# A mixture-of-experts stage on one core: a pair's 128 slots divided 32 and 96, with column tiles of 32, 32 and 64

## The reference

```python
grp = argmax(h @ w_grp + b_grp)                  # 4 groups of 8 experts
p_in, top_i = top_k(softmax(logits in the group), 2)
gate = p_grp * p_in / sum(p_in)
expert = grp * 8 + top_i                         # 2 experts of 32 for each of 256 tokens
# for each expert e, over the tokens sent to it (blocks padded to 128):
y = (silu(x @ w_gate[e]) * (x @ w_up[e])) @ w_down[e]     # 1024 -> 512 -> 1024
# the result of a token is the sum of its two experts' y, each times its gate;
# then a residual with a gain, and a last norm
```

## Time and profile before

| | us |
|---|---|
| median of 3 runs | 1170.4 |
| the profiled execution | 1173.7 |
| its span, first to last instruction | 1172.0 |
| PE busy (a matmul record counts from its start to its modelled end) | 1073.6 (92%) |
| PE weight loads | 606.6 (52%) |
| DVE busy | 399.2 (34%) |
| ACT busy | 169.7 (14%) |
| DMA, mean rate over the span | 263 GB/s |

### The profile page before, as it was taken

The page is one execution under the profiler, slowest core; times in us unless marked ns, Lnnn a source line. Parts: engine busy times, 40 slices in busy tenths (PEclk is TensorE's granted clock), DMA queues, the critical chain, the costliest instruction groups (busy, mean ns, idle before and its releaser), DMA issues.

```text
span 1172.0 us, 12847 instructions
## 1 busy us (share of the span) xinstructions
PE 1073.6 (92%) x5189; PEld 606.6 (52%) x5189; DVE 399.2 (34%) x735; ACT 169.7 (14%) x366; POOL 29.6 (3%) x88
## 2 busy tenths in 40 slices
PE   5999989789999999989977889999999988888885
PEld 4776877537666666478555363333333332232322
DVE  2857652404222222330033254443322222222223
ACT  1131330300000000010055000001011000000001
POOL 5300000000000000000000000000000000000000
PEclk9999965798999999999989979999999999999999
DMA  8442000065666666664410346999999999999993
GB/s 355 180 150 72 3 2 0 13 275 201 271 275 276 277 275 277 278 243 169 163 72 1 131 164 279 419 428 428 428 429 427 427 428 429 428 429 428 427 425 141
DMA packets 26816, 308.38 MB, mean 263 GB/s; under 512 B 6138, under 2 KB 6296, under 8 KB 7192
## 3 DMA queue, kind: packets, MB, share of 16 engines
q1 hardware_dynamic: 25308, 307.58, 63.4%
q10 hardware_dynamic: 1468, 0.24, 0.1%
HBM read 306.76 MB, written 1.05 MB: 263 GB/s over the span
## 4 chain that ended last, share of the span: by engine, by line
PE 75%; DMA 15%; DVE 6%; ACT 2%; issue 1%; SPq 0%; DVEq 0%
PE PS L1546 11%; PE PS L1005 11%; PE PS L1375 9%; PE PS L1389 9%; PE PS L1000 8%; DMA slot<-in_moe_w_up_dram 7%; PE PS L1592 7%; DMA AR<-in_moe_w_up_dram 4%; DMA XH<-in_moe_w_up_dram 4%; PE PS L1562 4%; PE PS L1232 2%; PE PS L1537 1%; PE PS L1174 1%; PE PS L1221 1%; PE PS L1480 1%; DVE AR L2013 1%
## 5 line engine op out<-in xcount | busy, mean ns | idle before, releaser
L1546 PE MATMUL PS<-slot,ATT 128*64 128x512 f32 (+1 forms) x672 | 142.7, 574 | 17.1 <-DMA slot<-in_moe_w_up_dram 12.5
L1375 PE MATMUL PS<-XH,slot 128*128 128x256 f32 x512 | 111.6, 379 | 0.0
L1389 PE MATMUL PS<-slot,AR 128*128 128x512 f32 x256 | 111.2, 592 | 0.0
L1375 PEld LDWEIGHTS PS<-XH,slot 128*128 128x128 f32 x512 | 97.3, 190 | 16.2 <-issue 3.3
L1546 PEld LDWEIGHTS PS<-slot,ATT 128*64 128x64 f32 x672 | 48.2, 137 | 110.0 <-issue 88.9
L1000 PE MATMUL PS<-XH,slot 128*128 128x256 f32 x432 | 96.0, 385 | 2.2 <-DVE XH L1694 1.2
L1000 PEld LDWEIGHTS PS<-XH,slot 128*128 128x128 f32 x432 | 83.3, 194 | 14.6 <-DVE XH L1694 1.6
L1389 PEld LDWEIGHTS PS<-slot,AR 128*128 128x128 f32 x256 | 48.6, 190 | 58.2 <-issue 57.9
L1546 PE MATMUL PS<-AR,ATT 128*64 128x512 f32 x320 | 72.0, 595 | 7.4 <-DMA AR<-in_moe_w_up_dram 5.0
L1592 PE MATMUL PS<-slot,MASKS 128*64 128x512 f32 x320 | 70.9, 595 | 1.3 <-DVE AR L2195 1.3
L1005 PE MATMUL PS<-slot,XH 128*128 128x256 f32 (+4 forms) x224 | 70.8, 475 | 0.0
(11 more groups left out here) (389 smaller groups left out, 1007.1 us busy)
## 6 DMA issues: line engine op xcount, KB each, us to landing
slot<-in_moe_w_up_dram SPq DMA_DIRECT2D x20, 2048.0 KB, 35.7
slot<-in_moe_w_down_dram SPq DMA_DIRECT2D x20, 2048.0 KB, 36.4
slot<-in_moe_w_gate_dram SPq DMA_DIRECT2D x18, 2048.0 KB, 32.7
slot<-in_w_ffn_dram SPq DMA_DIRECT2D x16, 2048.0 KB, 9.9
AR<-in_ada_w_dram SPq DMA_DIRECT2D x16, 1536.0 KB, 10.7
AR<-in_moe_w_gate_dram SPq DMA_DIRECT2D x11, 2048.0 KB, 36.3
AR<-in_moe_w_up_dram SPq DMA_DIRECT2D x9, 2048.0 KB, 35.0
AR<-in_moe_w_down_dram SPq DMA_DIRECT2D x9, 2048.0 KB, 30.6
```

The lines of the kernel that those rows point to most:

```text
L1375: ins = pe.matmul(PS[:, 2 * j + f // 2, (f % 2) * T:(f % 2 + 1) * T], slots[s][:, c * 512 + f * P:c * 512 + (f + 1) * P], HT[:, c, :], sta ...
L1389: ins = pe.matmul(PS[:, 4 + 2 * i + n, :], AT[:, j, f * T + i * P:f * T + (i + 1) * P], slots[s][:, f * D + n * 512:f * D + (n + 1) * 512] ...
L1546: ins = pe.matmul(PS[k * CAP:(k + 1) * CAP, bank_, 0:n], HS[:, c, k * CAP:(k + 1) * CAP], w[:, at:at + n], start=(c == 0), stop=(c == KC - 1))
```

## The change: what it does

- Of a pair's 128 slots, 32 (`FEW`) go to the expert with fewer tokens and 96 (`MANY`) to the other, and the smaller one always stands on the first side. Which one it is comes from a comparison of the counts on DVE (`SWAP`, and as integers `SIDE`). Pair 0 keeps 64 and 64 and its order.
- SP reads two sides for each pair from `SIDE` and fetches each unit in two DMAs, one for each side, 8 KB in each partition, so that the smaller expert's weights come into columns 0 to 2047 of the buffer. A unit's semaphore counts 32 for 16. Pair 0 and pair 1's units 10 and 11 are issued with the sides (0, 1) (pair 1's order is never changed: `swap[:, 0:2]` is cleared). SP waits once for `side_ready`, behind unit 11.
- DVE works out places, keys and gates in the order of the sides (`PLACE`, `KEYP`, `WTP`), ahead of pair 0's selections.
- PE does each step for pairs 1 to 15 in three matmuls: slots 0 to 31 with the first side's weights, 32 to 63 and 64 to 127 with the second side's (`SKEWED`). Each moves 512 columns.
- ACT copies 32 and 96 token columns for 64 and 64, and reads the two places after its wait for up.
- Further passes hold what goes over 32, 96 or (pair 0) 64, by 64s. The number of possible passes is 8 where it was 7.

```diff
 CAP = 64
+FEW, MANY = 32, 96
+NP = NE // 2
...
-        OVN = T * 2 // (CAP + 1)
+        OVN = 8
...
+            def pair_side(kind, half, pair, side):
+
+                src = kinds[kind][half].rearrange("q p (k n) -> q k p n", k=2)
+                return src[bass.ds(pair, 1), bass.ds(side, 1)].rearrange("q k p n -> p (q k n)")
+
+            def ring(u, g=0, sides=(0, 1)):
 
                 kind, half = u % UP // 2, u % 2
-                sp.dma_start(RING[u % NR], kinds[kind][half, bass.ds(PERIOD * g + u // UP, 1)].rearrange("q p n -> p (q n)"))\
-                    .then_inc(ring_loaded[u % NR], 16)
+                for k in range(2):
+                    sp.dma_start(RING[u % NR][:, k * HALF:(k + 1) * HALF], pair_side(kind, half, PERIOD * g + u // UP, sides[k]))\
+                        .then_inc(ring_loaded[u % NR], 16)
...
+            def pair_units(q, g):
+
+                sides = [sp.value_load(SIDE[0:1, bass.ds(2 * (PERIOD * g + q) + k, 1)], min_val=0, max_val=1) for k in range(2)]
+                for u in range(UP * q, UP * q + UP):
+                    ring_unit(u, g, sides)
+
+            for u in range(NR, 2 * UP):
+                ring_unit(u, 0, (0, 1))
+            sp.wait_ge(sems["side_ready"], 1)
+            for q in range(2, PERIOD):
+                pair_units(q, 0)
...
+            def expert_tokens(m):
+
+                few, many = place(2 * m), place(2 * m + 1)
+                act.activation(HS[:, :, 0:FEW], sorted_from(few, FEW), ACT.Copy)
+                act.activation(HS[:, :, FEW:P], sorted_from(many, MANY), ACT.Copy).then_inc(sems["hs_ready"], 1)
...
-                pe.wait_ge(ring_loaded[u % NR], 16 * (UP * PERIOD // NR * g + u // NR + 1))
+                pe.wait_ge(ring_loaded[u % NR], 32 * (UP * PERIOD // NR * g + u // NR + 1))
                 return RING[u % NR]
 
+            EQUAL = ((0, CAP, 0), (CAP, P, 1))
+            SKEWED = ((0, FEW, 0), (FEW, 2 * FEW, 1), (2 * FEW, P, 1))
+
+            def product(bank_, tiles, w, at, src, start, stop):
+
+                for r0, r1, k in tiles:
+                    ins = pe.matmul(PS[r0:r1, bank_, :], src[:, r0:r1], w[:, k * HALF + at:k * HALF + at + 512], start=start, stop=stop)
+                return ins
...
+                    for c in range(4 * half, 4 * half + 4):
+                        ins = product(4 + kind, tiles, w, c % 4 * EFF, HS[:, c, :], c == 0, c == KC - 1)
+                    ins.then_inc(sems[names[half]], 1)
...
+                            ins = product(6 + n, tiles, w, f * D + n * 512, AC[:, 2 * half + f, :], half == 0 and f == 0,
+                                          half == 1 and f == 1)
...
+            step(tt(swap, c_a, c_b, ALU.is_gt))
+            step(dve.memset(swap[:, 0:2], 0.0))
+            step(ts(kept, swap, -1.0, 1.0, ALU.mult, ALU.add))
+            dve.tensor_copy(ab(SIDE)[:, 0, :], swap)
+            dve.tensor_copy(ab(SIDE)[:, 1, :], kept).then_inc(sems["side_ready"], 1)
+            step(tt(d, s_b, s_a, ALU.subtract))
+            step(tt(d, d, swap, ALU.mult))
+            tt(ab(lo_hi)[:, 0, :], s_a, d, ALU.add)
+            step(tt(ab(lo_hi)[:, 1, :], s_b, d, ALU.subtract))
+            step(ts(lo_hi, lo_hi, float(HSS_AT), None, ALU.add))
+            dve.tensor_copy(PLACE[:, 0:NE], lo_hi).then_inc(sems["place_ready"], 1)
...
+            step(tt(dd, k_b, k_a, ALU.subtract))
+            step(tt(dd, dd, by(swap), ALU.mult))
+            tt(side_of(KEYP, 0), k_a, dd, ALU.add)
+            tt(side_of(KEYP, 1), k_b, dd, ALU.subtract)
+            for k, (x, y) in enumerate(((w_a, w_b), (w_b, w_a))):
+                step(tt(ww, y, by(swap), ALU.mult))
+                step(tt(side_of(WTP, k), x, by(kept), ALU.mult))
+                step(tt(side_of(WTP, k), side_of(WTP, k), ww, ALU.add))
...
-            selections(0).then_inc(sems["selw_ready"], 1)
+            selections(0, CAP).then_inc(sems["selw_ready"], 1)
...
-                selections(m + 1).then_inc(sems["selw_ready"], 1)
+                selections(m + 1, FEW).then_inc(sems["selw_ready"], 1)
```

More of the change, by code:

```diff
@@ L522, in _, with ring_unit @@
             ring(9)
-            def ring_unit(u, g):
+            def ring_unit(u, g, sides):
                 before = u - NR
                 sp.wait_ge(sems[released[before % UP]], PERIOD * g + before // UP + 1)
[L528 to L536, removed]
+                ring(u, g, sides)
+            def pair_units(q, g):
[7 more added lines that the diff above has]
+                pair_units(q, 0)
+            with sp.Fori(1, NP // PERIOD) as g:
+                for q in range(PERIOD):
+                    pair_units(q, g)
+            pair_units(0, NP // PERIOD)
             sp.wait_ge(sems["over_ready"], 1)
@@ L547, in _ @@
                         for half in range(2):
[L548 to L550 removed]
+                            sp.dma_start(OVER[kind][:, half * HALF:(half + 1) * HALF], pair_side(kind, half, pair_of, side))\
                                 .then_inc(sems[("over_gate", "over_up", "over_down")[kind]], 16)
@@ L928, in _ @@
             act.wait_ge(sems["place_ready"], 1)
-            at = places(1)
             act.wait_ge(sems["hss_filled"], KC)
-            expert_tokens(at)
-            with act.Fori(1, NE // 2 - 1) as m:
-                at = places(m + 1)
+            expert_tokens(1)
+            with act.Fori(1, NP - 1) as m:
                 expert_copies(m, EFF)
@@ L944, in _ @@
                     act.wait_ge(sems["up_filled"], x + NE // 2)
-                    expert_tokens(places(x + NE // 2))
+                    further_tokens(x)
                     expert_copies(x + NE // 2, EFF // 2)
@@ L1589, in project_back @@
                         for f in range(2):
[L1590 to L1593, removed]
+                            ins = product(6 + n, tiles, w, f * D + n * 512, AC[:, 2 * half + f, :], half == 0 and f == 0,
+                                          half == 1 and f == 1)
                     ins.then_inc(sems[("down_half", "down_filled")[half]], 1)
             pe.wait_ge(sems["first_low"], 1)
-            project(0, 0, 0, ("gate_half", "gate_filled"))
-            project(0, 0, 1, ("up_half", "up_filled"))
+            project(0, 0, 0, ("gate_half", "gate_filled"), EQUAL)
+            project(0, 0, 1, ("up_half", "up_filled"), EQUAL)
             pe.wait_ge(sems["sels_ready"], 1)
@@ L2108, in _ @@
             ins.then_inc(sems["sels_ready"], 1)
-            def selections(pair):
+            ab = lambda t: t.rearrange("p (q k) -> p k q", k=2)
+            side_of = lambda t, k: t.rearrange("p i (q k) -> p i k q", k=2)[:, :, k, :]
+            (c_a, c_b), (s_a, s_b) = ((ab(t)[:, 0, :], ab(t)[:, 1, :]) for t in (counts, first))
+            swap, kept = SWAP[:, 0, :], SWAP[:, 1, :]
+            d, lo_hi = E32[:, 4, 0:NP], E32[:, 5, 0:NE]
+            step(tt(swap, c_a, c_b, ALU.is_gt))
+            step(dve.memset(swap[:, 0:2], 0.0))
@@ new lines, in _ @@
+            k_a, k_b, w_a, w_b = (side_of(t, k) for t in (KEY, WT) for k in range(2))
+            by = lambda t: bc(t, 1, NT)
+            dd, ww = (E32[:, k, 0:NT * NP].rearrange("p (i q) -> p i q", i=NT) for k in (6, 7))
+            step(tt(dd, k_b, k_a, ALU.subtract))
[6 more added lines that the diff above has]
+                step(tt(side_of(WTP, k), side_of(WTP, k), ww, ALU.add))
@@ L2112, in selections @@
+            def selections(pair, few):
                 for i in range(NT):
[L2113 to L2116, removed]
+                    for k, (r0, r1) in enumerate(((0, few), (few, P))):
+                        ins = ts(SELW[:, i, r0:r1], IOTA[:, 0:r1 - r0], KEYP[:, i, bass.ds(2 * pair + k, 1)],
+                                 WTP[:, i, bass.ds(2 * pair + k, 1)], ALU.is_equal, ALU.mult)
@@ L2184, in further_experts @@
                 dve.tensor_copy(OVI[:, OVN + 1:2 * OVN + 1], side)
+                step(tt(first, first, CAPS, ALU.add))
                 step(stt(first, start, -float(CAP), first, ALU.mult, ALU.add))
```

84 lines of the change are left out of this document (47 added, 37 removed).

## The result

| | before | changed |
|---|---|---|
| median (lowest to highest) | 1171.5 us (1170.4 to 1176.7, 4 runs) | 1524.9 us (1522.6 to 1526.2, 4 runs) |
| ratio of the times, 95% interval | | 1.300 [1.295, 1.304] |
| span of the profiled execution | 1172.0 us | 1520.9 us |
| mean granted TensorE clock | 0.953 | 0.969 |

The account below looks back on a forecast made before the run. Transfers bound later pairs before, PE after: pair 1's start at 734.79, 15 pairs of 52.1 us (781.5), 5.1 to the scatter's end and 8.5 for the norm give a 1530 us span, forecast 1530 us, range 1154 to 1550.

Parts of the forecast that it names:

- What bounds it, before and after: Experts' stage: transfers set later pairs before at 29.4 us, PE having 4.4 us to spare; after the change PE is the bound.
- at half or less: Sign of being right: in the experts' stage the slices show DMA at half or less and PE near full.
- The step: PE's 32, 32 and 64 wide matmuls: 0.858 us becomes 1.99, unlike widths running apart, with 0.27 for changes; chance 0.62.
- The pair: PE, pairs 1 to 15: twenty-four steps, 47.7 us, plus 4.4 for scatter and turns, 52.1 us each.
- The start of pair 1: PE starts pair 1 at 734.79 us, taken from the profile before; the fifteen pairs are added to it.
- The tail: After the last down product: 5.1 us to the end of the scatter and 8.5 us for the last norm.
- The further pass: Extra pass for expert 21's tokens beyond 64, behind the last scatter: it goes, 15.9 us leave, reciprocal counts 16.
- The two transfers per unit: Each unit as two DMAs with 8 KB rows, 421 for 428 GB/s: +6.6 us if DMA stays the limit, bounds 0 to 10.
- DVE's tables: 20 more small DVE instructions before the first selections, 4.5 us, hidden in DVE's idle; at most 0.5 us late.
- (a): Rival, each of the 24 steps: widths mix freely, PE's pair stays 25.0 us, 1161 us in all (1154 to 1166); chance 0.30.
- (b): Rival, PE's steps: only two streams fit at a time, without drain; step 1.287, pair 35.3, 1277 us in all; chance 0.05.
- (c): Rival: a wrong count or side leaves one further pass in place while widths mix freely, 1177 us; chance 0.03.

## Why the prediction was right, step by step

- **What bounds it, before and after.** Right. Transfers bound the later pairs before; now PE does, no product waits for a DMA after 760 us, and the chain has DMA at 0%. One sign was set wrong: DMA "at half or less". The window shows a share of 0.65 at 242 GB/s, and the prediction's own pair, 12.58 MB in 52.1 us, is 241 GB/s, over half of 428.
- **The step.** 0.858 was to become 1.99 us; it is 1.985. The route was an inference from one row of another stage, where the tiles' rows differ; that a change of width alone acts the same was not known from it, and that its price came out the same to a hundredth of a us is in part luck. It is shown now, by four 32s (25.02 us a pair), a 32 beside a 64 (51.80) and the split into lost overlap, 0.86, and changes, 0.27 (1.715 and 0.27 were put at 1.716 and 0.27). The Trainium skill, TensorEngine Tiling (Array Packing), section Key Properties, says that a change of tiling mode drains the engine; 128x32 and 128x64 being two modes, the trace agrees: the streams of the two widths stand one after the other, and a change there and back costs 0.27 us.
- **The pair.** 52.1 us forecast, 51.93 measured: over fifteen pairs 2.6 us of the 9 by which the forecast of the span was high (1530 less 1520.9).
- **The start of pair 1.** Taken as 734.79, it was 728.2: the other 6.6 us. None of the change's parts lies before it except DVE's tables. The difference has opened in the early stages, before any changed instruction: the same instructions start 2.8 us earlier by 28 us into the span and 6.8 by 280. The version with four tiles of 32 has the same instructions up to there as the changed kernel, and its first exponential stands at 704.26, near the 705.13 of before and not the 698.81 of the changed kernel. So it belongs to the executions and not to the change.
- **The tail.** 13.6 us from the last product to the end; 1520.9 - 1507.2 (1491.25 + 15.95) = 13.7.
- **The further pass.** Sixteen reciprocals, as counted. Its 15.9 us lie in 10.5 to 16.6, measured alone, and the trace of that run shows them.
- **The two transfers per unit.** +6.6 forecast if DMA bounds; alone they gave 1.0052, 6.1 us (3.5 to 8.5). In the changed kernel they cost nothing, as PE bounds.
- **DVE's tables.** 4.5 us forecast, 3.7 measured (692.70 to the selections at 696.44). DVE's idle behind the selections shrank from 4.87 to 2.02 us and the idle before the product with up stayed 1.77: hidden.
- **The rivals.** (a), free mixing, fell; with four equal tiles its sum holds: 1161 us forecast for it, ratio 0.992, against 0.9937 [0.9912, 0.9963]. (b), two streams at a time, would have shown 35 us a pair, and four tiles of 32 run four loads at a time. (c) fell with the count of sixteen.

## What to carry to other kernels

Here, in float32 with tiles 32 and 64 wide, column tiles of TensorE ran side by side only among equals; other widths and types were not tried. Before mixing widths, cut the wide tile into tiles of the narrow width, which cost nothing per step here. Where a mix can't be avoided, group the matmuls by width, but expect the smaller part of the loss back (75 of 360 us here). And when a copy is split, split it along the row, not across the partitions.

## What the runs showed that was not expected

A copy over 64 of the 128 partitions moves at half the rate and keeps the DMA engines just as busy: 215 and 218 GB/s at a share of 1.01, against 428 and 426 for whole copies. The two halves, queued one behind the other, don't make it up.

The Trainium skill, SBUF — State Buffer, section Door 1: The DMA port swizzle, says that partitions 0 to 63 reach only eight of sixteen ports and gives about 218 GB/s for them; the trace agrees with the rate, and no run here shows the ports.

The share of busy DMA time does not tell full rate from half: 1.01 in both. The GB/s beside it does.

Two copies of 1 MB with 8 KB rows cost little against one of 2 MB with 16 KB rows: 420 to 422 GB/s against 426 to 428.
